# Prompt attention of a hybrid decoder step, rebuilt around pairs of heads

## The reference, cut to what matters

```python
o_cmp = softmax(q @ kc.T * scale - slope * dist) @ vc      # 31 compressed blocks
o_sel = softmax(q @ ks.T * scale - slope * dist) @ vs      # selected blocks: with 512 tokens, all of them
o_win = softmax(q @ kw.T * scale - slope * dist) @ vw      # window of 512: all of them here
o = g[0] * o_cmp + g[1] * o_sel + g[2] * o_win             # sigmoid gates per token and head
o_b = o * silu(g_b)
merged = gate_a * (o_a @ w_pa) + gate_b * (o_b @ w_pb)
```

## Time and profile before

| what | value |
|---|---|
| median of 3 runs | 2400.2 us (2392.92 to 2406.56) |
| profiled execution, its own time | 2398.52 us |
| its span from first to last instruction | 2396.6 us |
| PE multiplies busy | 2258.7 us, 94% |
| PE weight loads busy | 2083.9 us, 87% |
| DVE, ACT, POOL busy | 1229.3, 840.9, 268.5 us |
| mean granted PE clock | 0.973 |

### The profile page before, as it was taken

One profiled execution on the slowest core, in us unless ns is written; L12 is line 12 of the kernel. 1 busy time (PEld: TensorE's weight loads), 2 busy tenths in 40 slices (PEclk: granted clock), 3 DMA queues, 4 the chain that ended last, 5 costly groups with the idle time before them and its releaser, 6 DMA issues. The chain is left out here.

```text
span 2396.6 us, 53390 instructions
## 1 busy us (share of the span) xinstructions
PE 2258.7 (94%) x22058; PEld 2083.9 (87%) x22058; DVE 1229.3 (51%) x2440; ACT 840.9 (35%) x1647; POOL 268.5 (11%) x394
## 2 busy tenths in 40 slices
PE   7999999999999999999998899999889859999997
PEld 6998888888888888999998787889877659999997
DVE  6345555545555553488882445544145425355454
ACT  5333334333333422222222545454222224233342
POOL 0000000000000000010103324111215410000000
PEclk9999999999999999999999899999899879999999
DMA  4222121221212222786766223221859853445564
GB/s 158 93 77 75 51 65 57 64 80 55 74 52 64 73 70 64 258 292 217 255 199 190 61 72 79 72 83 48 287 168 322 286 194 108 135 146 167 186 200 141
DMA packets 143124, 320.00 MB, mean 134 GB/s; under 512 B 28090, under 2 KB 60068, under 8 KB 141860
## 3 DMA queue, kind: packets, MB, share of 16 engines
q1 hardware_dynamic: 102148, 225.64, 29.1%
q0 software_dynamic: 16912, 55.63, 7.1%
q10 hardware_dynamic: 23824, 35.33, 4.5%
HBM read 278.78 MB, written 46.06 MB: 136 GB/s over the span
## 5 line engine op out<-in xcount | busy, mean ns | idle before, releaser
L200 PE MATMUL acc<-xh,w_hi 128*128 128x272 f32 x2944 | 653.4, 303 | 12.9 <-DVE w_lo L168 11.9
L200 PE MATMUL acc<-xh,w_lo 128*128 128x272 f32 x2944 | 613.2, 290 | 0.0
L200 PE MATMUL acc<-xl,w_hi 128*128 128x272 f32 x2944 | 612.2, 290 | 0.0
L200 PEld LDWEIGHTS acc<-xh,w_hi 128*128 128x128 f32 x2944 | 462.7, 190 | 68.4 <-issue 45.4
L200 PEld LDWEIGHTS acc<-xl,w_hi 128*128 128x128 f32 x2944 | 467.0, 190 | 0.0
L200 PEld LDWEIGHTS acc<-xh,w_lo 128*128 128x128 f32 x2944 | 465.0, 191 | 0.0
L168 DVE TENSOR_TENSOR w_lo<-w_raw,w_hi 128x1024 fp32r<-128x1024 f32 x164 | 200.2, 1223 | 207.3 <-ACT w_hi L161 200.5
L161 ACT ACTIVATE w_hi<-w_raw 128x1024 fp32r<-128x1024 f32 x188 | 198.2, 1055 | 288.5 <-PE acc L200 196.0
L2814 DVE TENSOR_TENSOR m_w_lo<-m_w,m_w_hi 128x1024 fp32r<-128x1024 f32 x96 | 117.5, 1224 | 140.7 <-ACT m_w_hi L2749 140.7
L1305 DVE SCALAR_TENSOR_TENSOR b_C<-b_rows,b_pos_s,b_C 128x512 f32<-128x512 f32 x240 | 162.4, 744 | 0.0
L2939 PE MATMUL m_acc<-m_m_hi,m_w_hi 128*128 128x272 f32 x512 | 154.0, 301 | 0.0
(11 more groups left out here) (449 smaller groups left out, 3159.5 us busy)
## 6 DMA issues: line engine op xcount, KB each, us to landing
w_raw<-in_w_all SPq DMA_DIRECT2D x168, 512.0 KB, 3.5
m_w<-in_w_mo SPq DMA_DIRECT2D x96, 512.0 KB, 4.0
b_rows<-in_cmp_rows SPq DMA_DIRECT2D x128, 256.0 KB, 3.7
w_raw<-in_w_all ACTq DMA_DIRECT2D x20, 512.0 KB, 5.9
tmp_uT<-ub ACTq DMA_DIRECT2D x35, 272.0 KB, 3.2
m_gates<-tmp_uT SPq DMA_DIRECT2D x32, 272.0 KB, 2.7
d_ring<-in_sel_k SPq DMA_DIRECT2D x64, 128.0 KB, 4.5
d_ring<-in_sel_k POOLq DMA_DIRECT2D x64, 128.0 KB, 4.6
```

Of the source, the lines that this page charges most:

```text
L200: ins = self.nc.tensor.matmul(acc[:, c, 0:HALF], w[:, k % KH, :], x[:, k, c * HALF:(c + 1) * HALF], start=(k == 0 and m == 0), stop=(k == ...
```

## The change

A unit becomes a step `v`: one pair of heads (`p`), one tile of queries (`t`) and one branch (`v % 2`, selected or window); 64 steps, as many as units before, and 32 output units.

- `score(v)`: the two heads of the pair lie on the two row halves. The keys of each branch are loaded to both halves (`kT` doubles).
- The new `scales(v)` on DVE: reciprocal of the sums, product with the gates, and a scaling of the exponentials in place, before they are transposed. `turn(v)` waits for `scaled`, no longer for `exp_done`. ACT's two coefficients go.
- `values(u)`: the values are the stationary operand (64 columns) on the column half of the head, the transposed probabilities stream with 128 columns. All branches, the compressed one too, add up in one bank region with features on the partitions.
- `outs(u)`: one copy of 128x128 for two heads.
- The compressed scores use both row halves; their probabilities are scaled by `row_scales` before the transpose.
- The output goes to `obT` by features, stored a pair at a time. In the merge stage `turn_prompt` goes, and DVE multiplies the landed tile.
- POOL's `pool_dots` works in two halves, its operands fetched in two halves (`pool_fetch`), the state loads later, and the `U` jobs move to steps 28 to 34 and 42 to 48. SP loads group 1 behind the first weights.

```diff
@@ DVE
+            def scales(v):
+                p, t, k = v // 8, v // 2 % N_TILE, v % 2
+                j = v % 4
+                dve.wait_ge(exp_done, 2 * v + 2)
+                link(vec.reciprocal(inv[:, j, :], sums[:, j, :]))
+                c = 16 * (k + 1) + 2 * p
+                link(vec.tensor_tensor(coef[:, j, :], inv[:, j, :], gates[:, t, c:c + 2], ALU.mult))
+                for a in range(2):
+                    part = S[v % 2][:, a, 0:keys(v)]
+                    vec.tensor_scalar(part, part, coef[:, j, a:a + 1], None, ALU.mult).then_inc(scaled, 1)
+            def row_scales(w):
+                j = w % 4
                 dve.wait_ge(csum_ready, w + 1)
-                v.reciprocal(cinv[:, w % 2, :], csum[:, w % 2, :]).then_inc(cinv_ready, 1)
+                link(vec.reciprocal(cinv[:, j, :], csum[:, j, :]))
+                link(vec.tensor_tensor(cinv[:, j, :], cinv[:, j, :], gates[:, :, w], ALU.mult))
+                vec.tensor_tensor(Sc[j][:, :, :], Sc[j][:, :, :], cinv[:, j, :, None].to_broadcast([P, N_TILE, N_CMP_PAD]),
+                                  ALU.mult).then_inc(c_scaled, 1)
             def outs(u):
-                link(v.tensor_scalar(part[u % 2][:, :], o(0), inv[:, u % 4, 0:1], gates[:, t, 16 + w:17 + w],
-                                     ALU.mult, ALU.mult))
-                dve.wait_ge(coef_ready, u + 1)
-                link(v.scalar_tensor_tensor(out=part[u % 2][:, :], in0=o(1), scalar=coef[:, u % 4, 0:1],
-                                            in1=part[u % 2][:, :], op0=ALU.mult, op1=ALU.add))
-                v.scalar_tensor_tensor(out=out[g % 2][:, t, r, :], in0=o(2), scalar=coef[:, u % 4, 1:2],
-                                       in1=part[u % 2][:, :], op0=ALU.mult, op1=ALU.add).then_inc(ev_dve, 1)
+                vec.tensor_copy(out[p % 2][:, t * P:(t + 1) * P], bank[:, bank_of["O", u], 0:P]).then_inc(ev_dve, 1)
+            for v in range(NV):
+                p, step = divmod(v, 2 * N_TILE)
+                if v + 1 < NV:
+                    maxes(v + 1)
+                scales(v)
+                if v and v % 2 == 0:
+                    outs(v // 2 - 1)
+                dve.wait_ge(pe_jobs, done_at["T1", v])
+                vec.tensor_copy(PT[v % 2][:, 1, 0:keys(v)], bank[:, bank_of["T1", v], 0:keys(v)]).then_inc(ev_dve, 1)
@@ PE
+            def turn(v):
+                for a in range(2):
+                    b = job(f"T{a}", v)
+                    pe.wait_ge(scaled, 2 * v + a + 1)
+                    for n in range(v // 2 % N_TILE + 1):
+                        ins = nc.tensor.transpose(b[:, n * P:(n + 1) * P], S[v % 2][:, a, n * P:(n + 1) * P], T.ident[:, :])
                     done(ins)
             def values(u):
                 for k in range(2):
                     for n in range(t + 1):
-                        mm(b[:, k * HD:(k + 1) * HD], PT[u % 2][:, k, n * P:(n + 1) * P], vv[w // REP % 2][:, k, n, :],
-                           start=(n == 0), stop=(n == t))
-                done(mm(b[:, 2 * HD:3 * HD], PTc[w % 2][:, :, :].rearrange("p t q -> p (t q)"), vc[w // REP % 2][:, t, :],
-                        start=True, stop=True))
+                        for a, hp in enumerate(HALVES):
+                            mm(b[hp, 0:P], vv[g % 2][:, k, n, :], PT[k][:, a, n * P:(n + 1) * P],
+                               start=(k == 0 and n == 0), stop=False)
+                for a, hp in enumerate(HALVES):
+                    ins = mm(b[hp, 0:P], vc[g % 2][:, t, :], PTc[(2 * p + a) % 4][:, :, :].rearrange("p t q -> p (t q)"),
+                             start=False, stop=True)
+            for v in range(NV):
+                if v + 1 < NV:
+                    score(v + 1)
+                if v and v % 2 == 0:
+                    values(v // 2 - 1)
+                turn(v)
@@ merge_and_out
                 for c in turns_of(n):
-                    dve.wait_ge(tps, 2 + c + 1)
-                    v.tensor_tensor(o_raw[:, KW + c, 0:SEQ], turn[c % 2][:, :], gT[:, c, 0:SEQ], ALU.mult).then_inc(taken, 1)
+                    dve.wait_ge(ob_in[c // 4], 16)
+                    v.tensor_tensor(o_raw[:, KW + c, 0:SEQ], ob_t[:, c, :], gT[:, c, 0:SEQ], ALU.mult).then_inc(taken, 1)
```

More of the change, by code:

```diff
@@ L1563, in pool_dots @@
         n = 7 - 2 * s
[L1564 to L1571, removed]
+        p = self.prod[:, 0:n, :]
+        for k in range(2):
+            link(tt(p, self.Q8[:, 2 * s + 1:8, :], self.K8[:, k, s, None, :].to_broadcast([P, n, HD]), ALU.mult))
+            m = HD // 2
+            while m > 1:
+                link(tt(p[:, :, 0:m], p[:, :, 0:m], p[:, :, m:2 * m], ALU.add))
+                m //= 2
+            link(tt(self.D[:, k, s, 2 * s + 1:8], p[:, :, 0], p[:, :, 1], ALU.add))
     def pool_solve(self, link, s):
@@ L1643, in prompt_jobs @@
         if k in gaps:
-            at = START_PIECES + (gaps[k] + 1) * rest // (2 * NU)
+            at = START_PIECES + (gaps[k] + 1) * rest // (2 * NV)
         e = engine[job[0]]
@@ L1831, in background, with exps @@
                         highs[0] += 1
-            def exps(u):
-                w, t = divmod(u, N_TILE)
-                for k in range(2):
-                    background(place[f"S{k}", u])
-                    taken(act, (f"S{k}", u))
-                    f(S[u % 2][:, k, 0:keys(t)], S[u % 2][:, k, 0:keys(t)], ACT.Exp, scale=-1.0,
-                      bias=mx[:, u % 4, k:k + 1], accum_out=sums[:, u % 4, k:k + 1]).then_inc(exp_done, 1)
+            def exps(v):
+                for a in range(2):
+                    background(place[f"S{a}", v])
+                    taken(act, (f"S{a}", v))
+                    f(S[v % 2][:, a, 0:keys(v)], S[v % 2][:, a, 0:keys(v)], ACT.Exp, scale=-1.0,
+                      bias=mx[:, v % 4, a:a + 1], accum_out=sums[:, v % 4, a:a + 1]).then_inc(exp_done, 1)
             def row_exps(w):
@@ L2018, in row_turned @@
             def row_turned(w):
                 b = job("CT", w)
-                pe.wait_ge(c_exp, N_TILE * (w + 1))
-                done(nc.tensor.transpose(b[:, 0:P], Sc[w % 2][:, :, :].rearrange("p t n -> p (t n)"), T.ident[:, :]))
-            def score(u):
-                w, t = divmod(u, N_TILE)
-                banks = [job(f"S{k}", u) for k in range(2)]
-                for k, rows in enumerate((slice(0, HD), slice(HD, P))):
-                    done(mm(banks[k][:, 0:keys(t)], q[w % 2][rows, t * P:(t + 1) * P], kT[w // REP % 2][rows, 0:keys(t)],
-                            start=True, stop=True))
@@ new lines, in score @@
+            def score(v):
+                p, t, k = v // 8, v // 2 % N_TILE, v % 2
+                banks = [job(f"S{a}", v) for a in range(2)]
+                for b, hp in zip(banks, HALVES):
+                    done(mm(b[:, 0:keys(v)], q[p % 2][hp, t * P:(t + 1) * P], kT[p // 2 % 2][hp, k, 0:keys(v)],
+                            start=True, stop=True))
+            def turn(v):
+                for a in range(2):
+                    b = job(f"T{a}", v)
+                    pe.wait_ge(scaled, 2 * v + a + 1)
+                    for n in range(v // 2 % N_TILE + 1):
+                        ins = nc.tensor.transpose(b[:, n * P:(n + 1) * P], S[v % 2][:, a, n * P:(n + 1) * P], T.ident[:, :])
@@ L2970, in _ @@
                     turn_samples(1, ob_s)
-                for c in turns_of(n):
-                    turn_prompt(c)
                 if n >= 2:
```

337 lines of the change are left out of this document (158 added, 179 removed).

## The result

The changed kernel takes 2409.4 us (median of 20 runs, 2400.5 to 2416.5), the kernel before 2399.8 us (20 runs, 2392.4 to 2406.6): ratio 1.004, 95% interval 1.003 to 1.005. It is 9.6 us slower, which lies inside the 0.5% that I had called no change. The profiled execution has a span of 2409.0 us instead of 2396.6.

The account below looks back on a forecast made before the run. PE's list of work bounds the kernel, but a new wait on DVE's scalings returns most of its shortening. Terms -9 + 15 + 5 + 2 - 3.4 = +9.6 on 2400.2 give 2410 us, range 2364 to 2438.

Parts of the forecast that it names:

- PE's list: Attention stage: PE's own work gets about 5 us a pair of heads shorter, 40 us in all.
- The loop: Attention steps: transposes wait for DVE scalings, issued behind maxes that wait for new scores; of 40 us only -9 remains.
- The two kinds of pairs: Attention stage: pairs 0, 2, 4, 6 with pieces behind the transposes take 39.5 us, the others, pieces ahead, 36.1.
- Port waits: Attention stage: DVE's new SBUF products and scalings wait for POOL's operations, mainly 19 subtractions; +15 us.
- Clock: Attention stage: PE gaps in odd steps at 384 and 512 keys bring half clock; +5 us, ends 0 and 14.
- Start: Start of attention: earlier weight against second exponentials, more DVE operations and halved POOL dots; +2 us, ends -3 and 8.
- Merge: Merge stage: the 32 transposes of the prompt rows go from a full PE; -3.4 us.
- A: Attention stage: PE's list decides, DVE's chain being ready before the transposes; 2341 us, half of it 2370; 20%.
- B: Attention stage: the loop as forecast but no port and clock costs; 2390 us, 13%.
- C: Values jobs: the column halves don't overlap, 0.12 instead of 0.054 us an instruction; +45 us, 2455; 7%.
- D: Attention stage: half clock through much of pairs 0, 2, 4, 6, their 32 pieces at 3.0 us; +48, 2458; 6%.

Follow-up runs that it names:

- Experiment 1: Changed kernel with VectorE issuing the scalings of a step ahead of the next step's maxes: 2360.0 us, ratio 0.983.
- Experiment 4: Changed kernel with GpSimd's subtractions in the prompt attention stage writing 2 columns instead of 1024: 2384.4 us, ratio 0.993.
- experiment 2: Changed kernel with all projection pieces placed ahead of the transposes: 2370.5 us, ratio 0.988.
- experiment 3: Changed kernel with all projection pieces placed behind the transposes: 2462.8 us, ratio 1.026.
- experiment 6: Control: the kernel before with GpSimd's subtractions in the prompt attention stage cut to 2 columns: 2397.6 us, ratio 0.998.
- experiment 8: Changed kernel with scalings ahead of the next maxes, all pieces ahead of the transposes, and two-scalar scaling without the separate product: 2359.7 us, ratio 0.982.
- experiment 9: Changed kernel with scalings ahead of the next maxes and two-scalar scaling without the separate product, pieces left in place: 2357.1 us, ratio 0.981.
- experiment 11: Changed kernel with only the two-scalar scaling, which drops the separate product: 2398.3 us, ratio 0.998.
- experiment 7: Changed kernel with scalings ahead of the next maxes and values in the old form, probabilities loaded as weights: 2393.4 us, ratio 0.997.

## Why the prediction was right, and where its terms were off

The forecast was 2410 and +9.6 us; measured were 2409.4 and +9.6. The range held. I had given slower 0.43 and within 0.5% 0.31, with the border at 2412: the result is 0.4% and lies on the inner side of it. That the number fits to a microsecond is partly luck, since terms were off in both directions. Point by point:

- **PE's list, -40.** The windows give busy time 328.9 before and 301.3 after. Less half of the busy time at half clock (11.3 and 27.2) it is 317.6 and 274.1: -43.5. Experiment 1 gives the same by itself (290.0 - 16.2 = 273.8). The gain of the values part was overpriced (45; a run says 33, the timelines 40). By the timelines the rest, which I had at 5 us longer (compressed scores less, switches ahead of the scores more), came out 3.5 shorter; no run takes it apart.
- **The loop gives most of it back: right, and shown.** I had 31 us of the 40 eaten by the loop and 15 by waits on GpSimd, 46 in all; idle time grew by 46.6. Experiment 4 takes 15.9 us of it away (14.1 of 44.8, if all are cut at the first transposes of probabilities), which leaves 31 either way. Experiment 1 opens the loop by order alone and gets 49 us; experiments 2 and 3 move the cover and move the time both ways. The two kinds of pairs are in the trace.
- **Port waits, +15.** As idle time right (14 in the loop and 3 ahead of it), in full 21 us by experiments 4 and 6; the rest is busy time, most likely half clock that the waits bring. The place was half right: I expected single scalings of 1 to 2.4 us and a group mean well over 0.38; most of the waiting fell on the product ahead of them (mean 356 ns, longest 2194), and the scalings reached 1.1 us with a mean near 0.42. Only without the product (experiments 8, 9, 11) did scalings last 2.4 us and more.
- **Clock, +5: the term that was mis-sized.** It is +14 by the 44% that half clock costs a piece and at most +16 (half of 54.4 - 22.5), at my upper end of 14; with experiment 6 as the kernel before it would be near 12. Two to three times the term in any case. I had counted gaps of 1.8 us and over in odd steps from the earlier trace rows and not the gaps that the waits on GpSimd make: 44 waits, up to 4.2 us long. By experiment 4 some 6 or 7 of it hang on these.
- **Start, +2: not shown.** The first transposes of probabilities start 0.9 us later (1324.15 against 1323.26), but the first scores had started 2.3 us later, within their spread. From these scores on the start is 1.4 us shorter: PE waits 8.6 instead of 12.4 us ahead of the compressed transpose and then 1.9 for the first scaled probabilities.
- **Merge, -3.4.** Measured -3.5.
- **Not in the sum: the sample stage, -2.3.** Nothing in it was changed, and the kernel before with shortened subtractions takes 288.5 us there against its own 293.2, so the stage varies by more than that.

The terms as measured in the profiled executions, 31 + 16 + 16 - 43.5 for the stage, give 19.5, where the windows differ by 19. That they close is no proof of each: the first two are PE's idle time and the last two its busy time, parted by the half-clock estimate. A clock term some 7 to 11 us too small was met by a list 3.5 us shorter than forecast, by the sample stage's 2.3, and by the 2.8 us by which the profiled executions differ more than the medians (12.4 against 9.6): that is the luck in the number. The loop and the waits on GpSimd were forecast, and measured, near their size.

Of the rivals, A (PE's list decides) is what experiment 1 turns the kernel into: 2360, near the half-way figure of 2370 and not the full 2341, because 15 us of waits and more half clock than before remain. B (no port and clock costs) is refused by experiments 4 and 6. C is refused by the values group and experiment 7. D (half clock through much of four pairs) did not happen: 62 us of the stage are at half clock, in nine stretches. PE's idle time ahead of the transposes was forecast at 60 to 100 us and is 60.0; the values group at under 0.06 us an instruction and is 0.056; the stage at 5 to 25 us longer and is 18 to 19.

The Trainium skill (SBUF — State Buffer, Who interferes with whom) says that a VectorE instruction with two SBUF inputs, or in a two-port mode, contends with GpSimd, and one with a single SBUF input outside these modes doesn't. The runs agree: the reciprocal with one SBUF input never took over 163 ns, the product of two took up to 2194 (last section).

## What to carry to other kernels

When a change puts a new stage into a chain between two engines, write down the order in which each engine issues, and look for an operation that one engine issues just ahead of the one that waits: here one swap of two calls on VectorE was worth 49 us and turned 0.4% slower into 1.7% faster. Work used as cover hides one wait at a time, so moving it pays for one and uncovers another. Price a wait on the critical engine with what it does to the clock, and a VectorE operation that GpSimd can stretch by the longest neighbour on GpSimd, not by its own size.

## What the runs showed of the hardware

One VectorE operation is stretched by GpSimd and its neighbour isn't. Durations in the stage of the changed kernel, ns, least/median/most, by source line:

```profile
L1922 DVE RECIPROCAL a_inv<-a_sums x64: 153/160/163, 1322.7 to 1677.8; 128x2 f32<-128x2 f32 x64
```

```profile
L1924 DVE TENSOR_TENSOR a_coef<-a_inv,a_gates x64: 160/161/2194, 1322.9 to 1678.0; 128x2 f32<-128x2 f32 x64
```

The reciprocal reads one SBUF operand and never took over 163 ns in 64 times; the product of two, of the same size and right behind it, took up to 2194. The reductions with one PSUM and one SBUF operand stayed within 281 to 693 ns, which is their spread by size. A scaling of SBUF by a scalar took up to 1097 ns, and up to 3205 where it came first in line. So the size of such an operation says nothing of its price: a product of two elements a partition waited up to 2 us.

A second scalar in a scaling costs 0.06 us at all four widths here (two scalings take 0.60 instead of 0.48 us at 128 columns and 1.00 instead of 0.88 at 512), less than a separate product.
